# The experts' down-projection weights laid out by four adjacent rows per partition, with the gated activations written to match

## The reference, cut to what matters

```
def swiglu(h, w1, w3, w2):
    a = jax.nn.silu(jnp.einsum('bsd,df->bsf', h, w1)) * jnp.einsum('bsd,df->bsf', h, w3)
    return jnp.einsum('bsf,fd->bsd', a, w2)

def moe_swiglu(h, w_router, w1, w3, w2):
    ...
    for e in range(N_EXPERTS):
        y = y + gates[..., e:e + 1] * swiglu(h, w1[e], w3[e], w2[e])
    return y
```

## Time and profile before

| | us |
|---|---|
| median of 3 runs | 1457.12 |
| lowest and highest | 1455.85, 1460.83 |
| the profiled execution: its time | 1462.09 |
| the profiled execution: its span | 1460.3 |
| TensorE busy | 1441.4 (99%) |
| VectorE busy | 1133.1 (78%) |
| ScalarE busy | 944.8 (65%) |

### The profile page before, as it was taken

How to read it: one execution, slowest core, us unless ns; L and a number is a source line. 1 busy time by engine, 2 the same in 40 slices (tenths; PEclk the granted TensorE clock), 3 DMA queues, 4 the chain that set the end, 5 groups by cost and what they waited for, 6 DMA issues and landing times.

```text
span 1460.3 us, 19714 instructions
## 1 busy us (share of the span) xinstructions
PE 1441.4 (99%) x7542; PEld 1200.4 (82%) x7542; DVE 1133.1 (78%) x968; ACT 944.8 (65%) x844; POOL 35.4 (2%) x22
## 2 busy tenths in 40 slices
PE   9999999999999999999999999999999999999998
PEld 7998888888886787887888888888888888888886
DVE  6985664454476788988888898888888888898895
ACT  7633643443476766766777777777777777677774
POOL 0000000000000000000000001000000000000000
PEclk9999999999999999999999999999999999999999
DMA  9510666544542499999999999999999999999993
GB/s 360 206 58 28 237 220 219 191 172 146 176 162 83 152 362 364 386 364 348 377 368 386 391 373 380 372 375 376 386 383 372 387 393 367 386 389 372 369 391 149
DMA packets 183873, 437.21 MB, mean 299 GB/s; under 512 B 4880, under 2 KB 6416, under 8 KB 183824
## 3 DMA queue, kind: packets, MB, share of 16 engines
q1 hardware_dynamic: 180496, 426.11, 79.1%
q0 software_dynamic: 2336, 8.39, 2.1%
q10 hardware_dynamic: 992, 2.05, 0.4%
HBM read 431.29 MB, written 5.24 MB: 299 GB/s over the span
## 4 chain that ended last, share of the span: by engine, by line
PE 83%; issue 8%; DMA 4%; DVE 4%; ACT 1%; POOL 0%; DVEq 0%; ACTq 0%; SPq 0%; POOLq 0%
PE ps L272 26%; PE ps L274 25%; PE ps L273 25%; DMA raw<-in_od_moe_w 3%; DVE wlo L261 1%; PE ps L452 1%; DMA out<-arena,slot_tok 1%; ACT whi L255 1%; PE ps L991 1%; PE ps L840 0%; PE ps L1188 0%; DVE hTlo L316 0%; PE ps L2102 0%; DVE small L1418 0%; PE ps L333 0%
## 5 line engine op out<-in xcount | busy, mean ns | idle before, releaser
L261 DVE TENSOR_TENSOR wlo<-raw,whi 128x2048 fp32r<-128x2048 f32 x406 | 905.8, 2272 | 170.6 <-ACT whi L255 168.3
L255 ACT CAST whi<-raw 128x2048 fp32r<-128x2048 f32 x406 | 750.5, 1898 | 210.8 <-DMA raw<-in_od_moe_w 151.3
L272 PE MATMUL ps<-whi,hThi 128*128 128x512 f32 (+1 forms) x1240 | 490.2, 395 | 0.3
L274 PE MATMUL ps<-whi,hTlo 128*128 128x512 f32 (+1 forms) x1240 | 482.7, 389 | 0.0
L273 PE MATMUL ps<-wlo,hThi 128*128 128x512 f32 (+1 forms) x1240 | 482.5, 389 | 0.0
L274 PEld LDWEIGHTS ps<-whi,hTlo 128*128 128x128 f32 x1240 | 233.6, 188 | 48.7
L272 PEld LDWEIGHTS ps<-whi,hThi 128*128 128x128 f32 x1240 | 233.8, 189 | 47.3 <-issue 1.2
L273 PEld LDWEIGHTS ps<-wlo,hThi 128*128 128x128 f32 x1240 | 233.9, 189 | 45.8 <-issue 0.2
L272 PE MATMUL ps<-whi,aThi 128*128 128x512 f32 x560 | 219.3, 392 | 0.0
L274 PE MATMUL ps<-whi,aTlo 128*128 128x512 f32 x560 | 218.2, 390 | 0.0
L273 PE MATMUL ps<-wlo,aThi 128*128 128x512 f32 x560 | 217.9, 389 | 0.0
(11 more groups left out here) (308 smaller groups left out, 759.4 us busy)
## 6 DMA issues: line engine op xcount, KB each, us to landing
raw<-in_od_moe_w SPq DMA_DIRECT2D x168, 2048.0 KB, 9.6
raw<-in_ev_ffn_w SPq DMA_DIRECT2D x21, 2048.0 KB, 7.8
raw<-in_ev_w_in SPq DMA_DIRECT2D x6, 2048.0 KB, 13.1
raw<-in_ev_w_out SPq DMA_DIRECT2D x2, 2048.0 KB, 8.5
raw<-in_od_w_in SPq DMA_DIRECT2D x2, 2048.0 KB, 7.8
raw<-in_od_w_out SPq DMA_DIRECT2D x2, 2048.0 KB, 8.1
raw<-in_ev_w_in SPq DMA_DIRECT2D x2, 1024.0 KB, 8.6
xres<-in_x SPq DMA_DIRECT2D x2, 512.0 KB, 4.3
```

Source lines behind the costliest of these rows:

```text
L255: act.copy(whi[s][:, part], raw[s][:, part]).then_inc(hi_ready, 1)
L261: dve.tensor_tensor(wlo[s][:, part], raw[s][:, part], whi[s][:, part].bitcast(F32), ALU.subtract).then_inc(lo_ready, 1)
L272: pe.matmul(to, lhi, rhi, start=first, stop=False)
L274: return pe.matmul(to, llo, rhi, start=False, stop=last)
```

## The change

The view of `od_moe_w2` is changed so that partition p takes the four adjacent rows 4p to 4p+3 of a block in place of rows p, 128+p, 256+p and 384+p. In memory the four rows are one piece of 16 KB. The DMA for a w2 unit was built of 4 pieces of 4 KB for each partition, which lay 512 KB apart in memory, and is now one piece of 16 KB for each partition. The size of a unit, the buffers, the queue and the order of the loads are the same, and w1, w3 and the first layer's dense block are untouched.

Group c of the weights now holds the hidden columns 4i + c. The gate therefore reads its inputs in the old order, column 4i + c at a time, and writes column 4i + c to place c*128 + i of `actf`. Its two inputs are read side by side as before; its writes go round four places that are 512 bytes apart. Its shape is 96 partitions by 128 by 4, in place of 96 by 512. The transposes and the down product stay as they are. No instruction is added, removed or moved on any engine.

```
+        def by_row(t):
+            return t.rearrange("p (i c) -> p i c", c=FC)
+
+        def by_block(t):
+            return t.rearrange("p (c i) -> p i c", c=FC)
...
-        w2m = a["od_moe_w2"][0].rearrange("e (b c p) n -> (e b) p c n", p=P, c=FC)
+        w2m = a["od_moe_w2"][0].rearrange("e (b p c) n -> (e b) p c n", p=P, c=FC)
...
                 if tiles == 1:
-                    dve.tensor_tensor(actf[0:CAP, t, :], sil[0:CAP, t, :], H3[t][0:CAP, :], ALU.mult).then_inc(a_ready, 1)
+                    dve.tensor_tensor(by_block(actf[0:CAP, t, :]), by_row(sil[0:CAP, t, :]), by_row(H3[t][0:CAP, :]),
+                                      ALU.mult).then_inc(a_ready, 1)
...
-                    dve.tensor_tensor(actf[0:CAP, 0, :], sil_slots, H3[0][0:CAP, :], ALU.mult).then_inc(a_ready, 1)
+                    dve.tensor_tensor(by_block(actf[0:CAP, 0, :]), by_row(sil_slots), by_row(H3[0][0:CAP, :]),
+                                      ALU.mult).then_inc(a_ready, 1)
```

## The result

| | median | lowest to highest | runs |
|---|---|---|---|
| before | 1458.98 us | 1455.85 to 1465.07 | 8 |
| after | 1474.29 us | 1468.25 to 1480.2 | 8 |

The changed kernel takes 1.0103 times as long, 95% interval 1.0077 to 1.0128: 15 us slower. The forecast was 1456.6 us with a range to 1464.

A forecast was written before the change was run, and what follows sets the result against it. TensorE was taken as the bound, 16.87 us a step. From the median 1457.12 us, 0.5 us gained on w2 loads and 0 on the gate gave 1456.6 us; range 1452 to 1464 us.

The forecast's parts named there:

- the overlap: Nearly all 56 w2 savings of 0.19 us each were taken to be hidden under TensorE's work.
- these two places: TensorE's waits for the gate at 565.67 and 688.20 us, 1.53 and 2.18 us idle, costing 7.1 us together with slow clock.
- part 1: The w2 loads in 16 KB packets: a gain between 0.2 and 0.8 us, taken as 0.5.
- The price: A 16 KB packet of w2 should take 620 ns, making each w2 unit 4.96 us in place of 5.15.
- The sign that the prediction named for being wrong: The distance between experts' input transposes growing beyond 118.1 us, or one of TensorE's two waits missing.
- The rival on slow packets: 16 KB packets at 864 ns make DMA the bound, 17.69 us a step, 46 us more, 1503 us; chance 0.13.
- The gate: VectorE's gate with scattered writes: no extra time taken; upper bound 0.52 us more each, mostly hidden in VectorE's idle time.
- The rule of the Trainium skill: Engines access 16-byte SBUF lines and pay for each new line, so the gate would be dearer: 1457.8 us.
- The gather: The gather of the next expert's tokens on q0 was taken to lengthen the w1 loads before both TensorE waits.
- The two waits: TensorE's waits at the gate's transposes were to stay, 1.3 to 2.0 us each, with clock at 0.50 behind both.
- Forecast of the packets: Queue q1 was to have some 21,500 packets fewer, 56 x 384.

The follow-up runs named there:

- e1_pieces_alone: The kernel before with only the new w2 view (16 KB pieces) and the old gate: 1470.0 us, ratio 1.0063.
- e5_loads_alone: Only weight loads, computation left out, old view, 16 KB pieces and adjacent 4 KB rows: with two in flight the 16 KB stage is 2.34 us shorter in 12 steps.
- e8_gate_between: The kernel before with VectorE's gate moved ahead of the second half of the next w1: 1473.82 us, ratio 1.0114.
- e16_half_loads: The kernel before with each expert unit loaded in two 1 MB halves, each issued when its half buffer is free: 1454.1 us, ratio 0.9951.
- e2_gate_alone: The kernel before with only the new gate and the old 4 KB pieces: 1462.58 us, ratio 1.0007.
- e7_before_no_gather: The kernel before with each gather of tokens replaced by a plain load of 32 bytes a row: 1455.37 us, ratio 0.998.
- e14_rows_4KB_old_gate: The kernel before with four adjacent w2 rows per partition, reversed in the buffer as separate 4 KB packets, old gate: 1473.26 us, ratio 1.0074.
- e15_loads_paced_later: Only weight loads, issued 1.23 or 1.75 us late, with 8 KB pieces too: 16 KB stage 200.06 us at 1.23; every size slow at 1.75.
- e17_half_loads_rows: The kernel before with loads in two halves and four adjacent w2 rows per partition, 8 KB pieces, old gate: 1454.5 us, ratio 0.9955.
- e10_loads_paced: Only weight loads, each issued 0.69 or 1.23 us late: at 1.23 the 16 KB stage takes 199.10 us against 193.78 with the old view.
- e4_strided_transposes: The kernel before with 16 KB pieces, old gate, and TensorE's transposes reading every fourth column: 1473.98 us, ratio 1.0098.

## Why the prediction was wrong

**The step that failed** is the overlap: that the w2 loads reach "the end only at these two places", carried on in "Of the 56 savings almost all are hidden under TensorE" and in the sum of part 1, a gain of 0.2 to 0.8 us. Its premise was that a shorter w2 transfer can reach the end only as a gain. The price was right (615 ns in a full stream against 620). The effect on the other loads had no term at all: w1 lands 0.7 us later after the change (9.75 to 10.45 us on average), w1 had 0.3 us of room, and part 1 alone costs 9 us (e1_pieces_alone). The sign that the prediction named for being wrong is there: the distance of the experts grew from 118.1 to 120.1 us.

**Why the room was not seen.** I read "busy for 700.00 of 700.00 us" as a wide margin. It is a statement on whether there is slack and not on how much. The slack was to be had from rows that I quoted: the w1 load of 528.29 lands at 539.81 and its successor goes out at 546.58; 16.87 - 6.8 = 10.1 us; the loads on the chain took 11.52, 11.91 and 12.97.

**The rival on slow packets** named the right place ("Sooner if the queue can't be kept full") with a price that did not come. At 864 ns it would have given 1503 us; the 16 KB packets of the changed kernel take 0.645 us on the mean. But it also took the queue's room for too large. It put the three loads at 5.15 + 10.78 = 15.93 us of a step's 16.87. Back to back they take 193.85 / 12 = 16.15 us with the old view (e5_loads_alone), and queue q0 has its share beside them. From 560 to 1440 us of the kernel before:

```profile
q1 hardware_dynamic: 134312, 325.54, 99.2%
q0 software_dynamic: 1568, 5.51, 2.7%
```

By estimate that is 16.15 + 0.027 x 16.87 = 16.6 us, so the queue had some 0.3 us of a step to spare, and not 0.9, no more than the loop of the buffer had. With 16 KB pieces issued late, the three loads took 199.10 / 12 = 16.6 us without q0, so in the changed kernel the queue's rate and the landing of a single load can't be told apart as the bound. That the timing of the loads is what counts is shown by two kernels that move the same bytes from the same places: a w1 load issued 0.6 us later costs 14 us (e8_gate_between), loads issued earlier by halves gain 7 (e16_half_loads). The chance of 0.13 for this rival was all that spoke for a loss from part 1.

**The gate** has gone to 1.09 us, 0.42 us more and near the upper bound of 1.20; the value taken, none, was wrong, the nearest row (8 bytes apart) didn't bear on 512 bytes. The rule of the Trainium skill ("SBUF — State Buffer", its note on SBUF lines) had the direction right; whether the lines are the reason no run here shows. That VectorE's idle time hides it was right as far as the interval tells (e2_gate_alone, 1.0007, at most 1.0032).

**The gather** as the cause of both old waits is borne out (e7_before_no_gather). The two waits did not stay: the first grew from 1.53 to 2.44 us, with the low clock behind it as forecast, and the second is gone. No run shows why.

**Forecast of the packets.** 183873 - 162369 = 21504 = 56 x 384, as predicted, so the queue does send 16 KB as one packet.

**What stays open.** Adjacent rows in 4 KB packets lose 0.74% in the kernel (e14_rows_4KB_old_gate) and nothing in the loads alone (e5_loads_alone, e15_loads_paced_later). Runs show that the last DMA engines are the late ones, and that the loss disappears with room in the loop (e17_half_loads_rows, there in 8 KB pieces); they do not show what makes these engines late. For 16 KB the uneven finish of late loads is shown by itself (e10_loads_paced); how much of the kernel's 9 us is that and how much is the order of the rows isn't separated, and the rows alone would be enough. That the gate adds to the pieces more than it costs alone was argued and not measured.

## What to carry to other kernels

A bound engine that never waits may be a few tenths of a microsecond from waiting. Before a change of transfers, work out the loop of each buffer (landing, use, release, issue, landing), and what the queue needs for a period's loads back to back, and compare both with the period of the bound; if the room is smaller than the spread of the landings, a transfer that is cheaper in a full stream can still lose. Then make the room first: releasing and loading a buffer in halves gave more here than any layout of the rows, and with it the adjacent rows cost nothing.

## What the runs showed of the hardware

- A write of VectorE that jumps 512 bytes with each element costs 1.09 us for 96 x 512 f32, where writes side by side take 0.68: 0.8 ns more for an element (after against before).
- GpSimd's indirect DMA instruction beside that gate is longer too, though nothing of it was changed. The gather (L1769, the old L1762) of the changed kernel and its landing:

```profile
L1769 POOL DMA_INDIRECT arena<-xn_rows,slot_tok x7: 4774/4952/4982, 549.3 to 1270.6; - x7
...
DMA to landing us min/median/max: 12.2/12.6/13.3
```

  Before it was 2977 ns and 9.3 us. With the new gate alone (e2_gate_alone) the median is 4.8 us, with the pieces alone (e1_pieces_alone) 2.8. It cost no measurable time there.
- Weight loads of TensorE from every fourth f32 column take 218 ns in place of 140 (e4_strided_transposes against before).
- With 16 KB pieces among late loads (1.23 us) the sixteen counts of a load lie 1.9 us apart, with 4 KB 0.3 to 0.6 (e10_loads_paced); issued 1.75 us late, the old loads are uneven too, by 1.8 us (e15_loads_paced_later).
